# Hyena tail, output projection and experts' head of an encoder kernel: half of a finish moved to ScalarE and GpSimd, weight rounding moved ahead, idle products added, gate listing moved past a phase boundary

## What is computed

```python
for layer in range(DEPTH):
    hn = rms_norm(x, mix_norm[layer])
    if layer % 2 == 0:
        u = hn @ ev_w_in[j]
        y_att = diff_attention(u[..., :3 * D_ATT], ...)
        y_hy = hyena_mixer(u[..., 3 * D_ATT:], ...)     # rfft(z) * rfft(kern), irfft, + z * skip, * x1
        y = jnp.concatenate([y_att, y_hy], axis=-1) @ ev_w_out[j]
    else:
        u = hn @ od_w_in[j]
        y = mlstm_mixer(u, ...) @ od_w_out[j]
    x = x + y
    x = x + hier_moe(rms_norm(x, ffn_norm[layer]), ...)  # top-1 of 4 groups, top-2 of 8 experts
```

## Time and profile before

| what | value |
|---|---|
| median of 3 runs | 2549.4 us (2546.9 to 2549.99) |
| the profiled execution, its own time | 2544.74 us |
| its span in the trace | 2542.7 us |
| granted clock of TensorE, mean | 0.971 |
| PE busy | 2399.4 us, 94% |
| DVE, ACT, POOL busy | 73%, 57%, 19% |

### The profile page before, as it was taken

How to read it: one execution, slowest core, us unless ns; L and a number is a source line. 1 busy time by engine, 2 the same in 40 slices (tenths; PEclk the granted TensorE clock), 3 DMA queues, 4 the chain that set the end, 5 groups by cost and what they waited for, 6 DMA issues and landing times. The chain is left out here.

```text
span 2542.7 us, 32784 instructions
## 1 busy us (share of the span) xinstructions
PE 2399.4 (94%) x11738; PEld 1972.5 (78%) x11738; DVE 1847.5 (73%) x2211; ACT 1461.0 (57%) x1782; POOL 491.3 (19%) x433
## 2 busy tenths in 40 slices
PE   8989999897999999999998999997998999999997
PEld 6768877586777888888886877875887888888884
DVE  6838856667468998899884241378668999889893
ACT  6338843321316788788784241267425788888882
POOL 0001100101002433333320000026001333333331
PEclk9989999988999999999999999999998999999999
DMA  5110002110337999999994032022427999999997
GB/s 183 34 68 1 1 17 71 75 34 0 129 140 289 369 395 385 374 389 388 390 368 162 17 105 95 34 51 76 161 88 290 367 379 381 372 386 389 401 382 263
DMA packets 93944, 540.19 MB, mean 212 GB/s; under 512 B 19212, under 2 KB 31085, under 8 KB 68246
## 3 DMA queue, kind: packets, MB, share of 16 engines
q1 hardware_dynamic: 72102, 499.76, 50.4%
q0 software_dynamic: 19008, 33.61, 5.5%
q10 hardware_dynamic: 2736, 5.51, 0.6%
HBM read 519.37 MB, written 55.08 MB: 226 GB/s over the span
## 5 line engine op out<-in xcount | busy, mean ns | idle before, releaser
L2384 DVE TENSOR_TENSOR wL_rest<-ring,wH 128x2048 fp32r<-128x2048 f32 x384 | 868.9, 2290 | 115.4 <-ACT wH L2320 108.6
L2320 ACT CAST wH<-ring 128x2048 fp32r<-128x2048 f32 x384 | 729.5, 1911 | 145.0 <-DMA ring<-in_moe_w 114.1
L2194 PE MATMUL psum<-wH,xgH 128*128 128x512 f32 x1024 | 405.7, 396 | 7.0 <-DVE xgL L2384 6.7
L2196 PE MATMUL psum<-wH,xgL 128*128 128x512 f32 x1024 | 399.7, 390 | 0.0
L2202 PE MATMUL psum<-wL_rest,xgH 128*128 128x512 f32 x1024 | 275.3, 391 | 0.0
L2194 PEld LDWEIGHTS psum<-wH,xgH 128*128 128x128 f32 x1024 | 192.6, 188 | 47.2 <-DVE xgL L2384 8.9
L2202 PEld LDWEIGHTS psum<-wL_rest,xgH 128*128 128x128 f32 x1024 | 192.8, 188 | 40.5
L2196 PEld LDWEIGHTS psum<-wH,xgL 128*128 128x128 f32 x1024 | 192.8, 188 | 38.2
L2194 PE MATMUL psum<-wH,hidH 128*128 128x512 f32 x512 | 206.0, 402 | 3.9 <-DVE hidL L2384 3.9
L2196 PE MATMUL psum<-wH,hidL 128*128 128x512 f32 x512 | 200.2, 391 | 0.0
L2111 POOL COPY gidx<-slots 128x1 int32 (+1 forms) x60 | 70.5, 1174 | 497.0 <-PE psum L2211 497.0
(11 more groups left out here) (453 smaller groups left out, 4682.4 us busy)
## 6 DMA issues: line engine op xcount, KB each, us to landing
ring<-in_moe_w SPq DMA_DIRECT2D x192, 2048.0 KB, 9.5
ring<-in_ev_w_in SPq DMA_DIRECT2D x6, 2048.0 KB, 8.2
ring<-in_od_w_in SPq DMA_DIRECT2D x6, 2048.0 KB, 8.9
xnT<-in_moe_w SPq DMA_DIRECT2D x4, 2048.0 KB, 13.1
xn_scratch<-xn_route SPq DMA_DIRECT2D x14, 512.0 KB, 2.6
v_att<-in_x SPq DMA_DIRECT2D x8, 512.0 KB, 3.9
ring<-in_ev_w_out SPq DMA_DIRECT2D x2, 2048.0 KB, 7.7
xnT<-in_x SPq DMA_DIRECT2D x8, 512.0 KB, 3.4
```

The source lines that it names most:

```text
L2194: nc.tensor.matmul(psum[:, bank, :], xh[:, k, :], w3[0][:, n, cols], start=(half == 0 and n == 0), stop=False)
L2196: nc.tensor.matmul(psum[:, bank, :], xl[:, k, :], w3[0][:, n, cols], start=False, stop=False)
L2320: nc.scalar.copy(half_of(wH, b, e, c, half), raw(e, c, half)).then_inc(w_high, 1)
L2384: return nc.vector.tensor_tensor(out, whole, high.bitcast(F32), ALU.subtract)
```

## The change

There are three groups of edits.

1. In `hyena_transform` half c = 0 is no longer finished by VectorE. ScalarE, after its last spectrum copy, takes the four tiles out of PSUM with the scale, and GpSimd adds z and then multiplies by x1. ScalarE then rounds all eight parts of the output weights into a buffer that lies where `out_route` of layer 0 expects them, and VectorE subtracts the first part. TensorE does 80 idle products between `inverse(2)` and `inverse(3)`.
2. In `out_route` of layer 0 ScalarE's rounding and the first subtraction are gone, and the square root comes after the y roundings. In both layers SP loads one chunk at the end instead of two, and the 16 products for `slot_gate`, their copies and four small instructions on the totals leave the phase.
3. In `experts` SP loads the other chunk first; TensorE starts with the 16 products and 8 idle products, turns the rows, and does 8 more instead of 20 and 12; VectorE does the copies and small instructions at the head of `over_part(0)`; ScalarE's first `store_y` waits for them.

```diff
@@ out_route
+        def marks_at(layer):
+            at, gates_at = (0, 2) if layer else (6, 4)
+            A = xnL[:, at:at + 2, :]...
+            B = xnL[:, gates_at, :]...
+            return A, B
...
-                                for c in range(2):
-                                    if s0 + c + RING < S_END:
-                                        sp.wait_ge(proj, NT * 2)
-                                        load_chunk(sp, s0 + c + RING)
+                                sp.wait_ge(proj, NT * 2)
+                                load_chunk(sp, s0 + RING)
...
-                            last = nc.tensor.matmul(psum[:, 1, 0:NE], onesR[:], both[:, j, :], ...)
-                        last.then_inc(totalled, 1)
-                        pe.wait_ge(factors, 1)
-                        for n in range(16):
-                            last = nc.tensor.matmul(psum[:, WB, 0:2 * NE], A[...], B[...], ...)
-                        last.then_inc(listed, 1)
+                            nc.tensor.matmul(psum[:, LB, TOTAL:TOTAL + NE], onesR[:], both[:, j, :], ...)
...
-                        nc.scalar.activation(sd[:, 0:1], ones[:, 0:1], ACT.Sqrt)
+                        if not early:
+                            nc.scalar.activation(sd[:, 0:1], ones[:, 0:1], ACT.Sqrt)
                         def split_w(n):            # ScalarE
+                            if early:
+                                return
...
                         def split_w(n):            # VectorE
-                            dve.wait_ge(w_high, n + 1)
+                            if n < split_before:
+                                return
+                            if not early:
+                                dve.wait_ge(w_high, n + 1)
...
-                        weigh(1, gL[:]).then_inc(factors, 1)
-                        dve.wait_ge(totalled, 1)
-                        step(V.tensor_scalar(nov[:], psum[:, 1, 0:NE], ...))
-                        step(V.tensor_scalar(nov[:], nov[:], MAGIC, None, ALU.add))
-                        step(V.tensor_scalar(nov[:], nov[:], -MAGIC, 0.0, ALU.add, ALU.max))
-                        did(V.tensor_tensor_scan(incl[:, 1:NE + 1], ones[:, 0:NE], nov[:], 0.0, ALU.mult, ALU.add))
-                        dve.wait_ge(listed, 2)
-                        weights = psum[:, WB, 0:2 * NE].rearrange("p (f e) -> p f e", f=2)
-                        step(V.tensor_copy(slot_gate[:], weights[:, 0, :]))
-                        did(V.tensor_tensor(slot_gate[:], slot_gate[:], weights[:, 1, :], ALU.add))
+                        did(weigh(1, gL[:]))
@@ hyena_transform
                     # TensorE
                         inverse(2)
+                        pe.wait_ge(evacuated, 1)
+                        idle_products(back_bank(0, 0), 80)
                         inverse(3)
                     # ScalarE
+                        act.wait_ge(back, 8)
+                        for i in range(4):
+                            nc.scalar.activation(result_of(0, i)..., psum[:, back_bank(0, i), :],
+                                                 ACT.Copy, scale=hinv[:, i // 2:i // 2 + 1]).then_inc(evacuated, 1)
+                        for n in range(8):
+                            c = n // 4
+                            if n % 4 == 0:
+                                chunk_wait(act, S_OUT0 + c)
+                            nc.scalar.copy(wH[:, c, w_part(n), :], wide(S_OUT0 + c)[:, w_part(n), :]).then_inc(w_high, 1)
                     # VectorE
-                        finish(0)
-                        finish(1)
+                        dve.wait_ge(w_high, 1)
+                        did(rest_of(wide_rest(S_OUT0)[:, w_part(0), :], wide(S_OUT0)[:, w_part(0), :], wH[:, 0, w_part(0), :]))
+                        finish()                   # half c = 1 alone
                     # GpSimd
+                        pool_e.wait_ge(skipped, HC)
                         for n in range(2 * 4):
                             c, i = divmod(n, 4)
                             g = times(yT[:, 4 + 2 * c + i // 2, :], i % 2)
-                            pool_e.wait_ge(scaled, n + 1)
+                            if c == 0:
+                                pool_e.wait_ge(evacuated, i + 1)
+                                nc.gpsimd.tensor_tensor(result_of(0, i), result_of(0, i), times(z[:, i // 2, :], i % 2),
+                                                        ALU.add).then_inc(summed, 1)
+                                pool_e.wait_ge(summed, i + 1)
+                            else:
+                                pool_e.wait_ge(scaled, i + 1)
                             nc.gpsimd.tensor_tensor(g, g, result_of(c, i), ALU.mult).then_inc(added, 1)
@@ experts
+                        load_chunk(sp, s0 + 2)
...
-                        idle_products(OB, 20)
+                        marks, weights = marks_at(layer)
+                        for n in range(16):
+                            last = nc.tensor.matmul(psum[:, OB, 0:2 * NE], marks[...], weights[...], ...)
+                        last.then_inc(gates_listed, 1)
+                        idle_products(OB - 1, 8)
                         turn_x(0, 0, 0)
-                        idle_products(OB, 12)
+                        idle_products(OB - 1, 8)
...
+                            if first(e):           # store_y
+                                act.wait_ge(gates_ok, 1)
...
                             if e == 0:             # over_part
+                                dve.wait_ge(gates_listed, 1)
+                                step(V.tensor_copy(slot_gate[:], weights[:, 0, :]))
+                                V.tensor_tensor(slot_gate[:], slot_gate[:], weights[:, 1, :], ALU.add).then_inc(gates_ok, 1)
+                                step(V.tensor_scalar(nov[:], psum[:, OB, TOTAL:TOTAL + NE], ...))
+                                step(V.tensor_scalar(nov[:], nov[:], MAGIC, None, ALU.add))
+                                step(V.tensor_scalar(nov[:], nov[:], -MAGIC, 0.0, ALU.add, ALU.max))
+                                step(V.tensor_tensor_scan(ends, ones[:, 0:NE], nov[:], 0.0, ALU.mult, ALU.add))
```

More of the change, by code:

```diff
@@ L698, in attention, with out_route @@
                 end_phase()
+        TOTAL = 448
+        def marks_at(layer):
+            at, gates_at = (0, 2) if layer else (6, 4)
+            A = xnL[:, at:at + 2, :].rearrange("p c n -> p (c n)").rearrange("p (k j s) -> p k j s", k=2, j=NT)
+            B = xnL[:, gates_at, :].rearrange("p (n f e) -> p n f e", n=16, f=2)
+            return A, B
         @phase
-        def out_route(name, yT, hs, head_gain, s0, xsrc, xdst, layer, lists):
+        def out_route(name, yT, hs, head_gain, s0, xsrc, xdst, layer, lists, early=None):
             (tab_in, head_in, proj, added, y_high, y_rest, w_high, w_rest, squared, mean_ok, root_ok, recip_ok, xn_ok,
@@ L715, in t @@
                     return sb(st, f"{n}_route{name}", shape, dt)
-                plain, wH = sb_pair(st, f"w_high_route{name}", [P, 2, 8, HALF])
                 yH = t("y_high", [P, 2, KD, P], F32R)
                 yL = t("y_rest", [P, 2, KD, P], F32R)
+                ss, ms, sd, rs = (t(n, [P, NT]) for n in ("ss", "ms", "sd", "rs"))
+                if early:
+                    assert -(-nc.sbuf_base // 32) * 32 == early[1]
+                    t("w_room", [P, 2, 8, HALF])
+                    wH = early[0]
+                else:
+                    wH = t("w_high", [P, 2, 8, HALF], F32R)
                 g_bc = t("ffn_gain", [P, D])
                 xn = t("xn", [P, 2, D])
-                ss, ms, sd, rs = (t(n, [P, NT]) for n in ("ss", "ms", "sd", "rs"))
                 if hs is None:
@@ L971, in _ @@
                         for j in range(NT):
-                            last = nc.tensor.matmul(psum[:, 1, 0:NE], onesR[:], both[:, j, :], start=(j == 0), stop=(j == NT - 1))
-                        last.then_inc(totalled, 1)
-                        pe.wait_ge(factors, 1)
-                        for n in range(16):
-                            last = nc.tensor.matmul(psum[:, WB, 0:2 * NE], A[:, n // NT, n % NT, :],
-                                                    B[:, n, :, :].rearrange("p f e -> p (f e)"),
-                                                    start=(n == 0), stop=(n == 15))
-                        last.then_inc(listed, 1)
+                            nc.tensor.matmul(psum[:, LB, TOTAL:TOTAL + NE], onesR[:], both[:, j, :], start=(j == 0), stop=(j == NT - 1))
                     @block.scalar
                     def _(act):
-                        nc.scalar.activation(sd[:, 0:1], ones[:, 0:1], ACT.Sqrt)
+                        if not early:
+                            nc.scalar.activation(sd[:, 0:1], ones[:, 0:1], ACT.Sqrt)
                         def split_w(n):
                             c = n // PARTS
+                            if early:
+                                return
                             if n % PARTS == 0:
```

(20 more changed lines are left out.)

33 lines of the change are left out of this document (21 added, 12 removed).

## The result

| kernel | median of its runs | lowest to highest |
|---|---|---|
| before | 2549.0 us (6 runs) | 2543.2 to 2550.0 |
| after | 2559.7 us (6 runs) | 2555.0 to 2566.8 |

The account below looks back on a forecast made before the run. TensorE, busy 94% of the span, was taken as the bound, so only its idle or half-clock places could gain. +4.6 - 3.5 - 3.3 + 0.8 = -1.4 from 2549.4 gave 2548.0 us, range 2537.0 to 2552.5.

Parts of the forecast that it names:

- the first rows: Experts' head: gather from 761.4 lands a median 6.3 us later, at 767.7, just in time for TensorE's turn.
- the rows come late: Rival, chance 0.12: gather lands from 768.8 on, experts' head gives nothing in either layer; +5.4 us, 2554.8 us.
- the heads: Routing end and experts' head: TensorE's first product earlier, -3.5 us in layer 0 and -3.3 us in layer 1.
- the tail: Hyena tail to projection: GpSimd blocks VectorE, inverse(3) starts cold; +4.6 us after the head's 2.95 gain, bounds +1.7 to +7.4.
- the bookkeeping: Experts, VectorE: six small instructions, 1.35 us, of which 0.96 is absorbed by idle time; +0.4 per layer, +0.8 for two.
- the store of `xn`: Routing end: with one chunk load ahead, it lands near 758.5, before the slots at 760.41.
- seven conflicts: Hyena tail: seven of GpSimd's eight instructions each block VectorE for 1.2 us, 8.4 us in all, bounds 5.5 to 11.2.

Follow-up runs that it names:

- load_behind: Changed kernel, but SyncE issues the chunk load at the experts' head only once the first gather has landed; 2548.9 us, ratio 1.0011 to the kernel before.
- load_behind_hole: `load_behind` with VectorE's six small gate and totals instructions behind its first weight subtraction; 2546.8 us, ratio 1.0001 to the kernel before.
- tail_stand: Kernel before with early weight rounding, VectorE finishing half 0, GpSimd multiplying only behind VectorE's last turn, 100 idle products; 2545.0 us, ratio 0.9994.
- head_only: Kernel before with only the routing-end and experts'-head edits, hyena tail as before; 2550.5 us, ratio 1.0011 to the kernel before.
- best: `load_behind_hole` with the tail of `tail_stand`, and VectorE multiplying half 1 itself, so GpSimd has four multiplies; 2538.5 us, ratio 0.9966 to the kernel before.

## Why the prediction was wrong

**The failed step is that of the first rows.** The prediction had this as a rival, "the rows come late", at 0.12, with the right point of decision (a landing at 768.8 on), and put it aside with "the median is 6.3, and two loads are not in flight at once". Two loads are not, but one load and the gather are: it was the load's place in time, 0.8 us behind the gather's issue, that the sentence left out. `load_behind` shows it by a single wait. The forecast had -3.5 and -3.3 at the heads; after has +0.1 and +1.8 (B). These 8.7 us are most of the 12.1 between the forecast's -1.4 and the measured +10.7; the tail makes 1.4, the bookkeeping 1.0, and 1.0 is left over. In the forecast's own terms: "landing a median 6.3 us later" was 9.0 us in layer 0 and 9.4 in layer 1, and TensorE waited 2.90 and 3.37 us where the forecast had it arrive just in time. The rival itself, at 2554.8, was 5 us short: it let layer 1 come out even, where B is 1.8 longer, and it had the tail and the bookkeeping of the forecast.

**A number under it was off too.** The prediction let the store of `xn` land at 758.5 with one load ahead of it, before the slots. It lands 7.1 to 8.0 us behind its issue in layer 0, which in the kernel before would be 761 to 762, so the gather always starts behind the slots and close to the phase's end. That is why the two meet.

**What the moved gates are worth** was right in size in layer 0: -3.0 to -3.4 us in the six runs with the load behind the gather (forecast -3.5), once the rows are there. In layer 1 it is -1.5 to -2.4 (forecast -3.3). The forecast let the phase end with `weigh`; in layer 1 the store lands later, and in `load_behind` TensorE stands 2.42 us ahead of the 16 products instead of the 1.52 of layer 0. In `load_behind_hole`, where the store lands after 7.8 us, it stands 1.52 us in layer 1 too, and there the gain is the 2.4.

**The tail: right mechanism, one term too small.** Forecast were seven conflicts of 1.2 us, 8.4 in all, bounds 5.5 and 11.2; there are eight of 1.33, 10.65. All eight GpSimd instructions got in, one at each boundary between VectorE's. `inverse(3)` began at a clock of 0.50 as forecast and took 8.58 us for 9.45, the phase start was followed by the first product after 1.4 us as forecast, and the whole place is +6.0 (forecast +4.6, bounds +1.7 and +7.4). That ScalarE's roundings and the first subtraction cost nothing holds: in `tail_stand` they are there, and the last turn is late by the 0.7 us of VectorE's own finish ahead of it and no more.

**Bookkeeping:** forecast +0.4 per layer, since 0.96 us of idle time ahead of the second expert's subtraction would take the rest. It is +1.0 and +0.8, and `load_behind_hole` takes all of it away. The reserve was there: in layer 0 of `load_behind` VectorE's subtraction of the second expert's rows comes late, TensorE's second expert 1.1 us late, yet the subtraction of the earlier trace rows starts 14.63 us behind the first product, for 14.55 before, and VectorE no longer idles ahead of it. What the sum left out is the clock: it fell in TensorE's longer stand. Where it did not, C is +0.3 and +0.4 us, which is the forecast.

**The places' sum** for after is +9.7; its two results are +10.7 and +9.9. For `head_only` the places give -0.6 us and its runs +2.8 (interval 0 to 5.9). That its other executions lost the gather's race in layer 0, which its profiled one won, would explain it; with one profile this is only argued.

## What to carry to other kernels

A load moved out of a transfer's way helps only if it is put behind the next small transfer that somebody waits for, and that wants a wait on its landing: "later in the program" is not enough, and here 0.9 us behind the gather was still too near. Before counting an engine's idle time as a reserve, ask what the delay does to TensorE's stand and clock on its way there. And where a stall is taken away, add up the queue that stands behind it: in the tail both GpSimd's port and, without it, GpSimd's eight multiplies in a row set the end.

## What the runs showed of the hardware

A GpSimd instruction of about 1.5 us with two inputs in SBUF stopped VectorE for 1.33 us on the mean of eight, and where VectorE reads one input from PSUM not measurably (1.12 to 1.15 us beside GpSimd in `best`, 1.09 alone there and 1.14 in `after`). A gather that GpSimd began to issue 0.76 us ahead of a 2 MB load landed 0.19 us behind the load, 9.0 us after its issue, its first packet at 5.2 us; with the load held back its rows were there after 3.4 to 4.0 us (twelve places), its first packet at 1.8 to 2.4. The 80 idle products took 8.90 us; 12.9 us of standing behind them cost `inverse(3)` 1.4 to 2.1 us. Ahead of the second expert TensorE's granted clock stayed at 1.00 behind stands of 1.6 us, and fell to 0.50 behind stands of 1.9 to 2.9 us in ten places of twelve.
